# Prompt dilated attention: the first head pair's turned probabilities and values issued between the second pair's scores, the rest during its exchange of sums

## The reference: what is computed

```python
s = jnp.einsum('bqhd,bqjhd->bhqj', q, kg).astype(jnp.float32) * (HEAD_DIM ** -0.5)
s = jnp.where(valid[None, None], s, -jnp.inf)
lse = jax.nn.logsumexp(s, axis=-1)
p = jnp.exp(s - lse[..., None])
o = jnp.einsum('bhqj,bqjhd->bqhd', p.astype(v.dtype), vg)
...
w = jax.nn.softmax(jnp.stack(lses, axis=0), axis=0)
o = jnp.einsum('gbqh,gbqhd->bqhd', w.astype(outs[0].dtype), jnp.stack(outs, axis=0))
```

## Time and profile before

| | |
|---|---|
| median of 3 runs | 2180.66 us (2178.26 to 2182.61) |
| the profiled execution, its own time | 2182.8 us |
| its span in the trace | 2180.9 us |
| PE busy over the span | 1931.2 us (89%) |
| DVE, ACT, POOL busy | 994.8 us (46%), 586.5 us (27%), 117.4 us (5%) |
| the `pd` stage | from about 535 us, where its first DMA is issued, to 676.1 us, where the next stage's first DMA is |

### The profile page before, as it was taken

The page is one execution under the profiler, slowest core; times in us unless marked ns, Lnnn a source line. Parts: engine busy times, 40 slices in busy tenths (PEclk is TensorE's granted clock), DMA queues, the critical chain, the costliest instruction groups (busy, mean ns, idle before and its releaser), DMA issues. The chain is left out here.

```text
span 2180.9 us, 31611 instructions
## 1 busy us (share of the span) xinstructions
PE 1931.2 (89%) x11654; PEld 1623.8 (74%) x11654; DVE 994.8 (46%) x1960; ACT 586.5 (27%) x977; POOL 117.4 (5%) x211
## 2 busy tenths in 40 slices
PE   6999999997767755877886999999999999999995
PEld 5777779997444434544554888999999999999984
DVE  4302441000653854444445726545555555555545
ACT  4311001211844752333222213322222122212212
POOL 1000000000201003332000000000000000000000
PEclk9999999998977877999898999999999999999997
DMA  8654444112815209998563711110111011101102
GB/s 313 235 198 162 161 157 159 46 47 97 210 37 187 71 20 326 342 325 313 223 238 142 247 55 49 59 39 19 58 58 38 19 58 58 38 19 58 38 19 90
DMA packets 134188, 274.17 MB, mean 126 GB/s; under 512 B 23545, under 2 KB 75146, under 8 KB 130186
## 3 DMA queue, kind: packets, MB, share of 16 engines
q1 hardware_dynamic: 112570, 153.93, 21.4%
q0 software_dynamic: 21520, 118.91, 15.2%
HBM read 243.37 MB, written 79.10 MB: 148 GB/s over the span
## 5 line engine op out<-in xcount | busy, mean ns | idle before, releaser
L2053 DVE TENSOR_TENSOR tl_x<-tl_x,tl_ps 128x512 f32<-128x512 f32 (+1 forms) x198 | 135.8, 687 | 208.3 <-PE tl_ps L2210 208.3
L588 PE MATMUL tl_ps<-tl_T_lo,tl_up_hi 128*128 128x364 f32 (+1 forms) x1032 | 227.6, 329 | 0.0
L588 PE MATMUL tl_ps<-tl_T_hi,tl_up_lo 128*128 128x364 f32 (+1 forms) x1032 | 227.6, 329 | 0.0
L588 PE MATMUL tl_ps<-tl_T_hi,tl_up_hi 128*128 128x364 f32 (+1 forms) x1032 | 227.5, 329 | 0.0
L588 PEld LDWEIGHTS tl_ps<-tl_T_hi,tl_up_hi 128*128 128x128 f32 x1032 | 179.2, 188 | 1.4
L588 PEld LDWEIGHTS tl_ps<-tl_T_hi,tl_up_lo 128*128 128x128 f32 x1032 | 179.0, 188 | 0.0
L588 PEld LDWEIGHTS tl_ps<-tl_T_lo,tl_up_hi 128*128 128x128 f32 x1032 | 179.0, 188 | 0.0
L559 PE MATMUL fr_ps<-fr_w_hi,h_hi 128*128 128x512 f32 (+1 forms) x432 | 172.5, 399 | 0.0
L559 PE MATMUL fr_ps<-fr_w_lo,h_hi 128*128 128x512 f32 (+1 forms) x432 | 171.5, 397 | 0.0
L559 PE MATMUL fr_ps<-fr_w_hi,h_lo 128*128 128x512 f32 (+1 forms) x432 | 171.4, 397 | 0.0
L2210 PE MATMUL tl_ps<-tl_dn_hi,tl_f_hi 128*128 128x512 f32 (+1 forms) x396 | 156.5, 395 | 14.3 <-DVE tl_f_lo L2045 9.3
(11 more groups left out here) (262 smaller groups left out, 3248.7 us busy)
## 6 DMA issues: line engine op xcount, KB each, us to landing
sm_pages<-in_pool POOLq DMA_DIRECT2D x128, 256.0 KB, 4.7
sm_pages<-in_pool SPq DMA_DIRECT2D x128, 256.0 KB, 4.6
out_s<-in_cache POOLq DMA_DIRECT2D x8, 4080.0 KB, 21.1
tl_raw<-in_w_up SPq DMA_DIRECT2D x44, 512.0 KB, 4.7
fr_raw<-in_w_in POOLq DMA_DIRECT2D x9, 2048.0 KB, 9.7
sm_pages<-in_cache SPq DMA_DIRECT2D x16, 1024.0 KB, 9.4
zs<-fr_zt SPq DMA_DIRECT2D x48, 256.0 KB, 2.4
tl_dn_raw<-in_w_down SPq DMA_DIRECT2D x22, 512.0 KB, 3.6
```

What stands on the lines that cost most here:

```text
L588: last = pe.matmul(out[:, n * 512:n * 512 + b - a], lhs, rhs[:, a:b], start=(i == 0), stop=(i == len(pairs) - 1))
L2053: dve.tensor_tensor(x, x, dps[0:n, k * 512:k * 512 + 512], ALU.add).then_inc(added, 1)
```

## The change

It moves no data and adds no instruction to the work of a unit; it changes the order on three engines. `LAG` = 12 is new. On DVE, shares(0) now stands ahead of scores(36), the 13th unit of the second pair, and from there each scores(n) is followed by scale(n - 36). On PE, the same: from n = 36 on each scores(n) is followed by turn_probs(n - 36) and values(n - 37). On ACT, powers(0) stands ahead of exps(36), and each exps(n) is followed by move_probs(n - 36). The other twelve units of pair 0 (u = 12 to 23) follow behind the scores of pair 1 and ahead of shares(1), and then come the 24 units of pair 1 as before.

```diff
+        LAG = H // 2
...
         @block.scalar
...
-            for n in range(H, N):
+            for n in range(H, H + LAG):
                 exps(n)
-            for hp in range(2):
-                powers(hp)
-                for u in range(H):
-                    move_probs(hp * H + u)
+            powers(0)
+            for n in range(H + LAG, N):
+                exps(n)
+                move_probs(n - H - LAG)
+            for u in range(H - LAG, H):
+                move_probs(u)
+            powers(1)
+            for u in range(H):
+                move_probs(H + u)
...
         @block.vector
...
             for n in range(N):
+                if n == H + LAG:
+                    shares(0)
                 scores(n)
+                if n >= H + LAG:
+                    scale(n - H - LAG)
                 if n % QT == 2 and n >= QT:
                     log_sums(n // QT // 3 if n // QT % 3 else n // QT // 3 - 1, (n // QT - 1) % 3)
             log_sums(1, 2)
-            for hp in range(2):
-                shares(hp)
-                for u in range(H):
-                    scale(hp * H + u)
-                    if hp == 1 and u == 3:
-                        read_out(0)
+            for u in range(H - LAG, H):
+                scale(u)
+            shares(1)
+            for u in range(H):
+                scale(H + u)
+                if u == 3:
+                    read_out(0)
             read_out(1)
...
         @block.tensor
...
-            for n in range(H, N):
-                scores(n)
-            for n in range(N + 1):
+            for n in range(H, N + 1 + H + LAG):
                 if n < N:
-                    turn_probs(n)
-                if n >= 1:
-                    values(n - 1)
+                    scores(n)
+                u = n - H - LAG
+                if 0 <= u < N:
+                    turn_probs(u)
+                if u >= 1:
+                    values(u - 1)
```

## The result

The changed kernel took 2219.22 us in the median (4 runs, 2215.62 to 2221.52), the kernel before 2181.64 in runs beside it: ratio 1.017, 95% interval 1.0146 to 1.0193. The direction was as forecast, but 2219.2 lies just outside 2200 to 2218. The profiled execution took 2215.62 us with a span of 2213.8.

A forecast was written before the change was run, and what follows sets the result against it. Bound: pair 0's sums exchange, then PE's transposes and values. From 616.9, rounds 32.3, half-clock start 2.7, clock 4.5 reach 656.4; exchange 14.5 puts pair 1 at 670.9, +27.6 us: median 2208.3, range 2200 to 2218.

The forecast's parts named there:

- Step 1, the wait: DVE's shares(0) waits some 18 us for pair 0's sums at 612.45, twelve units behind it; start stays 615.23.
- Step 2, the round: Woven units on PE and DVE run serially, each the sum of its links: 3.01 us full clock, 4.38 half.
- the clock term of the woven part: Nine later woven rounds, PE at half clock 46% of the time: +4.5 us, bounds 0 and +12.3.
- Step 3, the second exchange: From pair 0's last log sum to pair 1's transposes: 14.5 us, PE standing some 4 us.
- three signs of being wrong: shares(0) well before 612; masks of units 37 to 47 under 2.5 us apart; pause before pair 1 gone or over 8.
- its tail: Whole kernel above 2217.1 us, from half clock all through and more lost behind it; chance 0.04.
- both slower rivals: Woven part: rounds overlap but the wait stays, 2188; or sums early but rounds serial, 2193.6; chance 0.05 each.
- the first rival: Woven rounds overlap at 1.66 us while the wait stays: pair 1 +7.5 us, 2188; chance 0.05.
- Overlapping rounds: Woven part: scores and masks run ahead, a unit costs only PE's own 1.66 us; 2188, chance 0.05.
- early sums: Pair 0's sums in at 597.7, woven part starting 14.7 us earlier, rounds serial: 2193.6; chance 0.05.
- the rival on that side: Faster kernel: woven rounds overlap at 1.66 us and start before 607.7; with sums early 2173.5; chance 0.02.

The follow-up runs named there:

- e3: Changed kernel with POOL's copies of new rows held back until pair 0's sums are loaded; ratio to the kernel before 1.0122, median 2208.22 us.
- e5: Kernel before, unwoven, with POOL's copies held back until pair 0's sums are loaded; ratio 0.9982, median 2180.22 us.
- e4: Changed kernel with four further unused transposes in each woven round, in PE's idle time; ratio to the kernel before 1.0096, median 2204.78 us.
- e2: Changed kernel with PE's scores one unit ahead of the transposes and DVE's scale ahead of its mask; ratio to the kernel before 1.0054, median 2193.03 us.
- e6: Changed kernel with both the uncoupled rounds of e2 and the held copies of e3; ratio to the kernel before 0.9974, median 2177.54 us.
- e8: Changed kernel with LAG 20, e2's order, copies held until pair 1's sums are loaded, powers(1) two units earlier; ratio to the kernel before 0.9954, median 2175.31 us.
- e1: Changed kernel with only shares(0) and powers(0) ahead of unit 36, nothing woven; ratio to the kernel before 1.0072, median 2196.92 us.

## Why the prediction was right and where it was wrong

**Step 1, the wait: right.** The sums came at 612.17, with shares(0) waiting for them, and twelve masks behind it. The wait was 14.9 us and not 18, because this execution's scores had run longer at half clock and DVE came later, at 597. That costs nothing, since the end of the wait is set by the DMA. e3 and e5 show that the copies cause the late loads. The arbitration rule that the prediction cited (the Trainium skill, DMA: Bandwidth & Descriptors, Queues, rings and completion order), read as I read it, would have had the stores land early; in these runs they did not as long as the copies were under way.

**Step 2, the round: right as a sum of links, wrong in the clock.** The links were 3.01 us at full clock by prediction and 2.99 in e4; at half clock 4.38 and 4.23 measured, since scores to mask took 0.85 and not 0.98. The step that failed is the clock term of the woven part, "I take the middle, 0.77, so 46% of the time at half clock", with its +4.5 us. The clock was 0.50 in all rounds, in both profiles and in e3, which makes the term its upper bound, +12.3; links that at half clock were 0.15 us shorter than the sum had them gave part of that back. The woven part ended at 661.2 where I had 656.4: 4.8 of the 5.4 us by which pair 1 came later than forecast. The two rows that I interpolated between the earlier trace rows were of other patterns of work; one of them was itself a mean over a stretch in which PE did all its work ahead of 602.8 and then stood.

**Step 3, the second exchange: right.** 15.1 us from the last log sum to pair 1's transposes (661.21 to 676.28) against 14.5: the stores landed 1.1 us sooner than in the row used for them, the loads 1.3 later. PE stood only 2.5 us ahead of pair 1 and not 4, because units 12 to 23 ran at a mean clock of 0.84 and took longer; the exchange decides here, so this cost nothing. None of the three signs of being wrong showed: shares(0) stood until 612.17, the masks came 3.0 us apart or more, and the pause was 2.5 us.

**The range.** The measured median is 10.9 us above the forecast of 2208.3, and the clock term is not the whole of it. 5.4 us are the later start of pair 1 (4.8 of them the woven part), which alone would have given 2213.7, inside the range. 1.0 us is the kernel before, whose median was 2181.64 beside the changed one and not the 2180.66 that I added to; in the later sets it was 2182.34, 2183.61 and 2186.49. The last 4.6 us are the difference between the timed loss (37.6) and the loss of the two profiled executions (33.0 and 32.9). The range had no term for that, and its cause is open (below). One sum in the prediction is also wrong: the forecast, its tail and both slower rivals are 0.84 + 0.04 + 0.05 + 0.05 = 0.98, not 0.95; less 0.04 of the first rival this gives the 0.94 stated.

**The rivals.** Overlapping rounds came only with e2's order, early sums only with e3's hold, and a weave was faster than before only with both (e6, e8), as the rival on that side said. But early sums gave a gain in the kernel before too, without any weave (e5). The Trainium skill's advice to interleave regimes (Perfetto Trace Analysis, Optimization Strategy) was not borne out by the order as changed, at +33 us. The two weaves that gained, e6 and e8, held the copies back too, and against e5 their stages are 2.2 us longer and 3.4 shorter, so no run here shows a clear gain from interleaving itself.

**Open.** The timed differences of e1, e2 and e3 are 5 to 8 us larger than those of their stages. Their profiled executions were among their quickest, and the others left no trace. The stage's start and what follows it vary by 2.5 and 9 us among the profiles, which is enough for it, but which of them it was is not shown. The mean granted clock points at its share of half clock: over the 28 executions of the kernel before that ran beside e5 to e8, those below 2180 us had 0.946 to 0.948, those above 2187 us 0.941 to 0.945.

## What to carry to other kernels

A weave of two streams over two engines needs one of them a step ahead. If engine A's step n + 1 is queued behind work that waits for B, and B's step behind A's, the round is the sum of all links, whatever each engine's busy share says; issue the first link one unit early. Before a wait is moved forward in a queue, count what it used to hide: here twelve units of exponentials, 9.4 us. A chain that leaves TensorE idle in every round can keep it at its low clock throughout, as here for 45 us; take that end of the bound, not the middle. And try the plain cause of a wait first: holding back the transfers that delayed the sums, one line, gave most of what the best version gained (6.9 of 10.3 us of the stage).

## What the runs showed of the hardware that was not expected

- TensorE, busy 67% of a stretch at half clock (30.26 of 45.20 us) in rounds with one pause of 1.3 us each, was granted 0.50 for all of it. Busy 92% (18.51 of 20.20 us), with pauses of 0.3 to 0.6 us, it came up after some 20 us (e4); with TensorE busy without a pause it came up after some 5 (e2, 617.9 to about 622.7).
- Once at full clock, the same rounds stayed there for 18 us with PE busy 76% (e4, 13.45 of 17.70).
- The last two stores of pair 0's sums, 4 KB each, had landed 2.8 us after their issue with the copies held back (e3, e5), and 18.7 us after it with the copies under way (before; 16.2 in the changed kernel).
